# Experts of a mixture layer: the down product with the weights stationary, its result transposed for the scatter

## The reference, cut to what matters

```
def swiglu(x, w13, w2):
    gate, up = jnp.split(x @ w13, 2, axis=-1)
    return (jax.nn.silu(gate) * up) @ w2
...
    logits = (t @ w_router).astype(jnp.float32)
    top_val, top_idx = lax.top_k(logits, TOP_K)
    top_w = jax.nn.softmax(top_val, axis=-1)
    for e in range(N_EXPERTS):
        gate_e = jnp.sum(jnp.where(top_idx == e, top_w, 0.0), axis=-1)
        out = out + gate_e[:, None] * swiglu(t, w13[e], w2[e])
```

## Time and profile before

| | |
|---|---|
| median of 3 runs | 3335.56 us (3332.74 to 3342.47) |
| the profiled execution | 3336.4 us, its span 3334.6 us |
| TensorE busy | 3143.5 us, 94% of the span |
| VectorE, ScalarE, GpSimd busy | 31%, 14%, 0% |
| the chain that ended last | PE 81%, DMA 9%, VectorE 6% |
| moved by DMA | 732.26 MB, mean 220 GB/s |

### The profile page before, as it was taken

The page is one execution under the profiler, slowest core; times in us unless marked ns, Lnnn a source line. Parts: engine busy times, 40 slices in busy tenths (PEclk is TensorE's granted clock), DMA queues, the critical chain, the costliest instruction groups (busy, mean ns, idle before and its releaser), DMA issues.

```text
span 3334.6 us, 56374 instructions
## 1 busy us (share of the span) xinstructions
PE 3143.5 (94%) x24078; PEld 2639.6 (79%) x24079; DVE 1017.2 (31%) x2224; ACT 481.1 (14%) x1090; POOL 15.6 (0%) x27
## 2 busy tenths in 40 slices
PE   5999999999999999999999988996879999999998
PEld 4888888888888888888888776885776787767874
DVE  5213322330230222434016354388231121121213
ACT  1001022110100101211001301016221011100110
POOL 0000000000000000000000000000000000000000
PEclk9999999999999999999999998998979999999999
DMA  8645634364374473436436336741247988889884
GB/s 331 261 164 215 236 121 179 143 243 173 136 286 180 175 267 139 171 127 252 170 139 249 115 148 258 301 165 77 97 168 280 358 330 322 312 310 356 330 315 185
DMA packets 55207, 732.26 MB, mean 220 GB/s; under 512 B 6593, under 2 KB 6777, under 8 KB 10533
## 3 DMA queue, kind: packets, MB, share of 16 engines
q1 hardware_dynamic: 51092, 716.68, 56.3%
q0 software_dynamic: 3984, 13.74, 1.2%
HBM read 729.31 MB, written 4.23 MB: 220 GB/s over the span
## 4 chain that ended last, share of the span: by engine, by line
PE 81%; DMA 9%; DVE 6%; issue 2%; ACT 1%; SPq 0%; DVEq 0%; ACTq 0%
PE psum L643 49%; PE psum L1073 11%; PE psum L1116 9%; DMA ring<-in_up_e_dram 3%; PE psum L630 3%; DVE ring L1481 3%; PE psum L700 2%; DMA ring<-in_up_dram 2%; DMA ring<-in_w_qk_dram 1%; PE psum L1097 1%; PE psum L1132 1%; DVE work L2033 1%; PE psum L712 0%; PE psum L723 0%; PE psum L682 0%
## 5 line engine op out<-in xcount | busy, mean ns | idle before, releaser
L643 PE MATMUL psum<-h_t,ring 128*128 128x256 f32 x5888 | 1289.1, 381 | 24.8 <-DVE h_t L1634 8.8
L643 PEld LDWEIGHTS psum<-h_t,ring 128*128 128x128 f32 x5888 | 1121.3, 191 | 191.4 <-issue 33.8
L643 PE MATMUL psum<-work,ring 128*128 128x256 f32 x2752 | 599.3, 380 | 8.8 <-ACT work L1288 3.7
L643 PEld LDWEIGHTS psum<-work,ring 128*128 128x128 f32 x2752 | 523.5, 191 | 82.9 <-issue 6.9
L1073 PE MATMUL psum<-h_t,ring 128*64 128x96 f32 x11264 | 471.6, 246 | 9.8 <-DMA ring<-in_up_e_dram 9.5
L1073 PEld LDWEIGHTS psum<-h_t,ring 128*64 128x64 f32 x11264 | 467.0, 137 | 13.6 <-issue 12.4
L1116 PE MATMUL psum<-ring,work 128*96 128x512 f32 x704 | 304.1, 593 | 0.0
L1481 DVE SCALAR_TENSOR_TENSOR ring<-ring,cond 128x1024 f32<-128x1024 f32 x240 | 279.2, 1221 | 8.2 <-DMA ring<-in_ada_dram 7.4
L1116 PEld LDWEIGHTS psum<-ring,work 128*96 128x96 f32 x704 | 114.1, 163 | 184.1 <-issue 182.8
L1544 DVE TENSOR_TENSOR work<-work,psum 128x256 f32<-128x256 f32 (+1 forms) x118 | 49.7, 421 | 626.9 <-PE psum L643 611.9
L2325 DVE TENSOR_TENSOR work<-work,psum 128x256 f32 x176 | 74.2, 421 | 407.5 <-PE psum L1073 407.5
(11 more groups left out here) (330 smaller groups left out, 1569.9 us busy)
## 6 DMA issues: line engine op xcount, KB each, us to landing
ring<-in_up_e_dram SPq DMA_DIRECT2D x64, 2048.0 KB, 7.9
ring<-in_ada_dram SPq DMA_DIRECT2D x60, 2048.0 KB, 7.8
ring<-in_up_dram SPq DMA_DIRECT2D x55, 2048.0 KB, 8.0
ring<-in_down_e_dram SPq DMA_DIRECT2D x32, 1792.0 KB, 8.4
ring<-in_down_dram SPq DMA_DIRECT2D x20, 2816.0 KB, 9.8
ring<-in_up_e_dram SPq DMA_DIRECT2D x32, 1536.0 KB, 8.7
ring<-in_down_e_dram SPq DMA_DIRECT2D x16, 2048.0 KB, 8.8
ring<-in_w_qk_dram SPq DMA_DIRECT2D x12, 2048.0 KB, 9.0
```

The costliest lines, as they stand in the source:

```text
L643: mm = pe.matmul(half(b), w, moving(k, j * lin.groups + m), start=(k == 0), stop=(k == depth - 1))
```

## The change

The down product is turned around, as the up product already was: the weights are stationary, in two halves of 64 columns where the expert has at most 96 tokens, and `mid` moves. The 8 by 22 tiles are run in two rounds of four groups; each round is three chunks of 30, 30 and 28 tiles. The banks of the groups are 3, 0, 1, 2. The result has the outputs on the partitions, so ScalarE copies each of the eight groups into `y_out`, TensorE transposes them back into banks 4 and 5 (6 and 7 for a second list), and VectorE and ScalarE copy these into `y_pos` as before. The scatter then uses banks 0 to 3 in place of 4 to 7. The layout of the weights in memory changes with it, outside the timed program.

```
-        "upE": Rounds(4, (4, 4, 3), DT, "up_e"), "downE": Sides((0, 8, 15, 22), "down_e"),
-        "scatter": uses(b4=2, b5=2, b6=2, b7=2),
+        "upE": Rounds(4, (4, 4, 3), DT, "up_e"), "downE": Blocks(2, LIN, FT, (0, 30, 60, LIN * FT), "down_e"),
+        "turn": {"turned": 2, "free4": 1, "free5": 1, "free6": 1, "free7": 1},
+        "scatter": uses(b0=2, b1=2, b2=2, b3=2),
...
+        self.banks = [(LIN - 1 + m) % LIN for m in range(groups)]
...
+        y_out = tiles(72, DT)
...
-                for side in range(2):
-                    src = dram[down.source][p.of("of " + down.source, side)]
-                    for part, (lo, hi) in enumerate(zip(down.edges, down.edges[1:])):
-                        slot, use = p.slot(side * down.parts + part)
+                with sp.Fori(0, down.rounds) as i:
+                    src = dram[down.source][p.of("of " + down.source, 0, i, 1)]
+                    for c, (lo, hi) in enumerate(zip(down.edges, down.edges[1:])):
+                        slot, use = p.slot(c, i)
...
-                for b in range(LIN):
-                    if b not in [bank_of for _, bank_of, _, _ in late] or b < lists:
-                        pe.wait_ge(bank_free[b], reads(p, b))
-                for side in range(2):
-                    for part, (first, last) in enumerate(zip(down.edges, down.edges[1:])):
-                        slot = chunk_landed(p.slot(side * down.parts + part))
-                        if side == 0 and part == down.parts - 1:
-                            for _, b, _, _ in late:
-                                pe.wait_ge(bank_free[b], reads(p, b))
-                        for n in reversed(range(lists)):
-                            for k in range(first, last):
-                                mm = pe.matmul(bank(2 * side + n)[0:slots(n), :],
-                                               mid[:, k, n * P:n * P + slots(n)],
-                                               ring[:, slot, (k - first) * 512:(k - first + 1) * 512],
-                                               start=(k == 0), stop=(k == FT - 1))
-                        mm.then_inc(chunk_done[slot], 1)
+                columns = ((0, P // 2), (P // 2, P)) if width <= NARROW else ((0, P),)
+                with pe.Fori(0, down.rounds) as i:
+                    for n in range(down.groups * FT):
+                        m, k = n // FT, n % FT
+                        b = down.banks[m]
+                        if k == 0:
+                            pe.wait_ge(bank_free[b], reads(p, b, 0, i, 1))
+                        if n == FT - len(late):
+                            for _, late_b, _, _ in late:
+                                pe.wait_ge(bank_free[late_b], reads(p, late_b))
+                        if n in down.edges:
+                            first = n
+                            slot = chunk_landed(p.slot(down.edges.index(n), i))
+                        w = ring[:, slot, (n - first) * P:(n - first + 1) * P]
+                        for lo, hi in columns:
+                            mm = pe.matmul(half(b)[lo:hi, 0:width], w[:, lo:hi], mid[:, k, 0:width],
+                                           start=(k == 0), stop=(k == FT - 1))
+                        if n + 1 in down.edges:
+                            mm.then_inc(chunk_done[slot], 1)
+                        elif k == FT - 1:
+                            mm.then_inc(bank_full[b], 1)
+
+                p_turn = place("turn", e)
+                for f in range(DT):
+                    b, side = down.banks[f % LIN], f // LIN
+                    pe.wait_ge(bank_free[b], reads(p, b, side) + 1)
+                    for n in range(lists):
+                        into = LIN + side + 2 * n
+                        if f % LIN == 0:
+                            pe.wait_ge(bank_free[into], reads(p_turn, into))
+                        mm = pe.transpose(bank(into)[0:slots(n), f % LIN * P:(f % LIN + 1) * P],
+                                          y_out[:, f, n * P:n * P + slots(n)], ident[:, :])
+                    if f % LIN == LIN - 1:
+                        mm.then_inc(signal["turned"], 1)
...
                 for f in range(DT):
-                    b, side = LIN + f % LIN, f // LIN
+                    b, side = f % LIN, f // LIN
...
+                for f in range(DT):
+                    b = p.what.banks[f % LIN]
+                    act.wait_ge(*block_end(p, f % LIN, f // LIN))
+                    act.activation(y_out[:, f, :], half(b), ACT.Copy).then_inc(bank_free[b], 1)
+                p = place("turn", e)
                 for side in range(2):
-                    slot, use = p.slot((side + 1) * p.what.parts - 1)
-                    act.wait_ge(chunk_done[slot], use + 2)
-                    act.activation(y_pos[:, 1, side * 512:(side + 1) * 512], bank(2 * side + 1),
-                                   ACT.Copy).then_inc(bank_free[2 * side + 1], 1)
+                    act.wait_ge(signal["turned"], p.of("turned", side + 1))
+                    act.activation(y_pos[:, 1, side * 512:(side + 1) * 512], bank(LIN + 2 + side),
+                                   ACT.Copy).then_inc(bank_free[LIN + 2 + side], 1)
...
-                    dve.wait_ge(chunk_done[slot], use + 2)
-                    dve.tensor_copy(y_pos[:, 0, side * 512:(side + 1) * 512], bank(2 * side)).then_inc(bank_free[2 * side], 1)
+                    dve.wait_ge(signal["turned"], p.of("turned", side + 1))
+                    dve.tensor_copy(y_pos[:, 0, side * 512:(side + 1) * 512], bank(LIN + side)).then_inc(bank_free[LIN + side], 1)
...
-        "down_e": cat([by_row(w) for w in a["moe_w2_2"][0]]),
+        "down_e": cat([by_tile(w, LIN) for w in a["moe_w2_2"][0]]),
```

More of the change, by code:

```diff
@@ L124, in counts, with __init__ @@
         return c
-class Sides:
-    def __init__(self, edges, source):
-        self.source, self.edges, self.parts = source, edges, len(edges) - 1
+class Blocks:
+    def __init__(self, rounds, groups, depth, edges, source):
+        self.rounds, self.groups, self.depth, self.edges, self.source = rounds, groups, depth, edges, source
+        self.banks = [(LIN - 1 + m) % LIN for m in range(groups)]
     def counts(self):
-        return {"chunk": 2 * self.parts, "of " + self.source: 2, **{f"free{b}": 1 for b in range(LIN)}}
+        c = {"chunk": self.rounds * SLOTS, "of " + self.source: self.rounds}
+        for b in self.banks:
+            c[f"free{b}"] = self.rounds
+        for b in self.banks[:-1]:
+            c[f"full{b}"] = self.rounds
+        return c
 class Made:
@@ L531, in round_end, with block_end @@
             return bank_full[b], products(p, b, k + after * p.what.per_full[b], i, p.what.per_full[b])
+        def block_end(p, m, i):
+            if m == p.what.groups - 1:
+                slot, use = p.slot(SLOTS - 1, i)
+                return chunk_done[slot], use + 2
+            b = p.what.banks[m]
+            return bank_full[b], products(p, b, 0, i, 1)
         def gathered(f):
@@ L567, in stream_rounds, with stream_blocks @@
                         sp.dma_start(ring[:, slot, 0:hi - lo], src[:, lo:hi]).then_inc(chunk_in[slot], 16)
-            def stream_sides(p):
+            def stream_blocks(p):
                 down = p.what
-                for side in range(2):
-                    src = dram[down.source][p.of("of " + down.source, side)]
-                    for part, (lo, hi) in enumerate(zip(down.edges, down.edges[1:])):
-                        slot, use = p.slot(side * down.parts + part)
+                with sp.Fori(0, down.rounds) as i:
+                    src = dram[down.source][p.of("of " + down.source, 0, i, 1)]
+                    for c, (lo, hi) in enumerate(zip(down.edges, down.edges[1:])):
+                        slot, use = p.slot(c, i)
                         sp.wait_ge(chunk_done[slot], use + 1)
-                        sp.dma_start(ring[:, slot, 0:(hi - lo) * 512], src[:, lo * 512:hi * 512]).then_inc(chunk_in[slot], 16)
+                        sp.dma_start(ring[:, slot, 0:(hi - lo) * P], src[:, lo * P:hi * P]).then_inc(chunk_in[slot], 16)
             for part, times in stages():
@@ L584, in _ @@
                         stream_rounds(place("upE", e))
-                        stream_sides(place("downE", e))
+                        stream_blocks(place("downE", e))
                 elif times > 1:
@@ L1122, in expert @@
-                y_side = lambda b: reads(p, b) + 1
+                columns = ((0, P // 2), (P // 2, P)) if width <= NARROW else ((0, P),)
[19 more added lines that the diff above has]
+                            mm.then_inc(bank_full[b], 1)
@@ L1125, in expert @@
                 for f in range(DT):
-                    b, side = LIN + f % LIN, f // LIN
+                    b, side = f % LIN, f // LIN
                     if f % LIN == 0:
                         for n in range(lists):
-                            pe.wait_ge(bank_free[2 * side + n], y_side(2 * side + n))
```

(13 more changed lines are left out.)

## The result

The kernel after takes **3403.84 us** (median of 4 runs, 3397.27 to 3407.40) against 3336.53 us of the kernel before (4 runs): ratio 1.0197, interval 1.0183 to 1.0210. It is slower by 2.0%.

A forecast was written before the change was run, and what follows sets the result against it. TensorE's own time was taken to bound the experts, with DMA not far behind. Terms -67.7 + 14.8 + 4.8 + 49.2 + 5 + 28 + 6 = +40.1 us gave 3376 us, range 3283 to 3400.

The forecast's parts named there:

- The down product: Each expert's down stage: 704 records in 29.48 us replace 37.94 us, saving 8.46 us, -67.7 us for eight.
- transfers: Weight DMAs in the down stage: demand of 391 GB/s loses 0.6 us an expert, +4.8 us for eight.
- reading on: Straight-line code in the expert loop: some five more blocks an expert at 0.15 us each, +6 us (0 to 12).
- The turn: Transposing the down output back: eight transposes at 0.23 us, 1.85 us an expert, +14.8 us; their waits 0.
- Banks: Next gather no longer waits for VectorE's last sum of bank 7: 0.51 us in six passages, -3.1 us.
- The code: Expert loop: a turn touches ten instruction blocks where eight stay, so both jumps miss every turn; about two in three.
- Jump ahead and back: Misses at the expert loop's jumps: ahead 6 x 8.2 = +49.2 us and +5 us at the end; back +28 us.
- Up: Up stages: the ring is full at the next up stage, as now; no separate up term in the sum.
- the loop still fits: Rival on the expert loop: its code stays, no packets after the second expert; -51.2 us, 3285 us; chance 0.22.
- The transfers become the bound: Rival on the expert stages: code fits but DMA limits them; -38 us, 3298 us; chance 0.08.
- Only the jump ahead misses: Rival on the expert loop: the block of the loop's start survives; +12 us, 3348 us; chance 0.08.

The follow-up runs named there:

- e6: Kernel after with the down product in four rounds of two groups (less code), plus 82 instructions of waits at the program's start: 3321.63 us, ratio 0.9961.
- e5: Kernel after without the wide branch in TensorE's program, plus 82 instructions of waits moving the expert loop to a block border: 3283.89 us, ratio 0.9852.
- e2: Kernel before with 250 matmuls (1000 instructions) that never run behind its wide branch: 3346.18 us, one execution.
- e3: Kernel before with 24 matmuls (96 instructions) that never run, jumped over inside the narrow branch between up and down: 3419.17 us, one execution.
- e9: e6 without the 82 instructions at the program's start: 3399.97 us, ratio 1.0196.
- e1: Kernel after with the wide branch left out of TensorE's program alone: 3300.44 us, ratio 0.9887.
- e12: Kernel after with 850 matmuls (3400 instructions) that never run behind its wide branch, 20564 instructions in all: 3370.79 us, ratio 1.0107.
- e11: Kernel before with 1000 matmuls (4000 instructions) that never run behind its wide branch, 20564 instructions in all: 3329.41 us, ratio 0.9985.
- e7: Kernel before with 150 matmuls (600 instructions) that never run behind its wide branch, 17164 instructions as after the change: 3354.74 us, ratio 1.0061.
- e4: Kernel before with 12 matmuls that never run, jumped over inside the narrow branch between up and down: 3361.65 us, one execution.
- e10: e6 with eight instructions fewer in the narrow branch and 24 matmuls that never run behind the wide branch: 3319.74 us, ratio 0.9954.
- e8: Kernel after with 100 matmuls (400 instructions) that never run behind its wide branch, 17564 instructions in all: 3383.97 us, ratio 1.0146.

## Why the prediction was right or wrong

The direction and the mechanism held: slower, since the loop's code no longer stays. The time came 28 us above the forecast and 4 us above the top of the range. Step by step:

- **The down product**: 704 records at 240.1 us / 5632 = 42.6 ns, 30.0 us, not 29.48. With its waits a stage took 31.1 us; forecast were 29.5 + 0.6 + 0.75 for transfers and reading on. The stages before took 37.84 us on average, where I had taken one of 37.94. -53.7 against -56.9 us.
- **The turn**: I priced a transpose at 0.23 us by the nearest row; eight took 1.08 us. They have 96 stationary columns where those of the output have 128; that this is the reason was not tested. A wait of 0.35 us for VectorE's copy came in, that I had put at 0: the cover, 1.85 us of transposes, was shorter than I thought. Together 1.4 us instead of 1.85. The forecast took a row of another shape as the price.
- **Banks**: the wait for VectorE's last sum is gone, as forecast, but the 0.51 us are not won where the wide branch is kept: in e6's passages that read nothing the transposes still start after 0.47 to 0.53 us, now for "issue". Only where there is no branch to jump over do they start after some 0.3 us (0.24 to 0.31 in e5).
- **The code**: right in kind. The rows left a store of 8 to 27 blocks; I took eight at two in three, and e2 against e3 shows eight: no packet from 2640 to 3200 us against 44, and e2's loop stays with its 2926 instructions, since a turn touches eight blocks. That the oldest block is the one that goes, which makes both jumps miss in every turn, no row showed and it was my assumption; it fits what came, 10 or 11 packets between one down stage and the next in the kernel after and nine of nine in e3 and e9, and no run tested the order. Where the blocks stay, a jump back reads nothing: the up loop's in the kernel before (no packet after the second expert began), and all of e5's from 2600 to 3200 us.
- **Jump ahead and back**: the sum had 8.2 + 4 + 1.85 us over the earlier trace rows; seven passages grew by 92.0 us, where the sum gave 13.0 + 49.2 + 28 = 90.2. That the total agrees so well is partly luck, since two errors offset each other: the turn was cheaper (9.9 us instead of 13.0), the jumps dearer (82.1 instead of 77.2). A passage has 10.94 us of idle time against 6.28 with the jump ahead alone, so the jump back adds 4.7 us, not 4; alone, in e1, it costs 6.76.
- **Up**: +5.0 us, forecast 0. The chunks are waited for 10.9 us against 9.5. Reading the code again is not shown to be the reason: e12 reads as many packets in each turn, and its eight up stages took 479.3 us, against 480.8 of the kernel before.
- **The step that failed** is none of the terms but what the sum left out: that all ahead of the experts stays as it was. It put that part at nothing without saying why. That part took 20.2 us more in the profiled run, from waits for the ring (36.3 us against 14.7, all such waits ahead of the experts added up). Without it the sum stands at +48 against +40 forecast, some 3384 us and inside the range, and at equal length of the programs (e12 against e11) the change costs 41 us. That the 20 us come and go with the program's length and not with the change is shown by e7 and e12; by what mechanism is open.
- **The rivals**: "the loop still fits" was priced at -51 us; e5, which makes it true by leaving out the wide branch, has -49 in the median and -60 in the experts. Some 8 of the 60 us are the stall of the first passage, which goes with the branch; what is left is close to the price. "The transfers become the bound": not in the kernel after, which waits 7.7 us in its down stages, nor in e5, at 88.9%; e6 with its smaller chunks waits 17 us there. "Only the jump ahead misses" did not occur.

## What to carry to other kernels

Count the blocks of instructions that one turn of a loop touches, the block read ahead behind each run of code and the block of the loop's end included, and keep them within what stays (here eight of 256: none was read again in e2, nine of nine in e3, whose turn runs through seven). In this kernel a float32 product of two halves left eight records (5632 of matmuls and as many weight loads for the 8 x 176 tiles of the down product), and the branch that is never taken cost the two blocks read at the jump over it, since the loop's end lies there: two packets in the kernel before at 2554.4 to 2564.2. Where a loop is near that edge, a few instructions or the loop's place against a border decided some 80 us here, so look at the instruction queue in the profile before and after any change to the code's size. And compare a stage by its own rows: a shift of 20 us in stages that nobody touched came along with the program's length here.

## What the runs showed of the hardware that was not expected

- Twenty-four matmuls that never run made a kernel 2.5% slower (3419.17 us in one execution, against 3334.65), as the turn's nine blocks are all read again (e3, nine packets in each turn), where eight stayed (e2, none from 2640 to 3200); 82 instructions of waits at the start of the program, that pad it to a border, undo such a loss (e9 to e6, 3399.97 to 3321.63 us).
- Reading again can come and go from turn to turn when the end of a run of code lies 28 or 23 instructions ahead of a border (e1 and e4, with nine packets between some down stages and the next and none between others); at 39 and more it did not (39 in e6, 47 in e10, no packet from 2640 to 3200 in either; 73 in the kernel before, none from 2565 to 3330).
- With the length of TensorE's program the waits for weights in unchanged stages moved (loop begun at 2434.5 us in e11, 2444.3 before, 2465.8 in e7, 31 us apart); not by the length alone, since e2 and e8 have the same and are 9 us apart; why is open.
- A passage with 11 us of idle time is paid twice: the granted clock was 0.69 on average over it, and the 32 products of the gather at its end took 5.68 us instead of 3.71.
